# Feed-forward by seven products for each two-by-two block, with its inner activations held in DRAM

## What is computed

```python
hn = _rmsnorm(h, norm_ffn_w[l])
h = h + jnp.square(jax.nn.relu(hn @ w_ffn_in[l])) @ w_ffn_out[l]
...
return _rmsnorm(h, norm_final_w)
```

## Time and profile before

| | |
|---|---|
| median of 3 runs | 2551.32 us (2548.46 to 2555.57) |
| the profiled execution | 2553.9 us, of which the trace's span is 2552.1 us |
| granted TensorE clock over the span, share of full speed | 0.972 |
| PE, PEld busy | 2441.5 us (96%), 2077.6 us (81%) |
| DVE, ACT, POOL busy | 1002.2, 723.1, 689.7 us |
| instructions | 33188 |
| DMA | 232.11 MB, mean 91 GB/s |

### The profile page before, as it was taken

The page is one execution under the profiler, slowest core; times in us unless marked ns, Lnnn a source line. Parts: engine busy times, 40 slices in busy tenths (PEclk is TensorE's granted clock), DMA queues, the critical chain, the costliest instruction groups (busy, mean ns, idle before and its releaser), DMA issues.

```text
span 2552.1 us, 33188 instructions
## 1 busy us (share of the span) xinstructions
PE 2441.5 (96%) x13182; PEld 2077.6 (81%) x13182; DVE 1002.2 (39%) x1479; ACT 723.1 (28%) x1147; POOL 689.7 (27%) x423
## 2 busy tenths in 40 slices
PE   6999996899898999999999999999999999999997
PEld 5788886899876888888888877988888788887886
DVE  4176634455535312212213344123333343557533
ACT  4144554122412100101101121135443113655022
POOL 2221112343322433333334322321111231111321
PEclk8999997899898999999999989999999999999998
DMA  6722212322330111111111115523441346524422
GB/s 206 205 58 67 67 51 68 92 57 57 133 107 25 58 50 42 49 49 49 49 49 49 47 35 187 169 62 91 120 118 51 130 165 145 134 65 149 149 91 91
DMA packets 257967, 232.11 MB, mean 91 GB/s; under 512 B 43233, under 2 KB 228359, under 8 KB 256312
## 3 DMA queue, kind: packets, MB, share of 16 engines
q1 hardware_dynamic: 234680, 170.65, 23.7%
q10 hardware_dynamic: 23168, 59.81, 6.5%
HBM read 167.41 MB, written 65.11 MB: 91 GB/s over the span
## 4 chain that ended last, share of the span: by engine, by line
PE 92%; DVE 2%; ACT 1%; DMA 1%; issue 1%; POOL 1%; POOLq 0%; ACTq 0%; DVEq 0%; SPq 0%; PEldq 0%; PEld 0%
PE PS L282 40%; PE PS L301 18%; PE PS L1828 4%; PE PS L2478 3%; PE PS L418 3%; PE PS L1783 3%; PE PS L2034 2%; PE PS L1320 2%; PE PS L1326 2%; PE PS L698 1%; PE PS L2023 1%; PE PS L2317 1%; PE PS L676 1%; PE PS L1337 1%; PE PS L686 1%
## 5 line engine op out<-in xcount | busy, mean ns | idle before, releaser
L253 POOL CAST Wh<-Wraw 128x1024 fp32r<-128x1024 f32 x144 | 150.8, 1047 | 1469.0 <-PE PS L282 619.3
L255 POOL TENSOR_TENSOR Wl<-Wraw,Wh 128x1024 fp32r<-128x1024 f32 x144 | 375.6, 2608 | 20.7
L1702 ACT ACTIVATE rbuf<-PS 128x1024 f32<-128x1024 f32 x32 | 32.9, 1028 | 493.7 <-PE PS L282 483.2
L282 PE MATMUL PS<-Fl,Wh 128*128 128x512 f32 x512 | 157.6, 389 | 0.0
L282 PE MATMUL PS<-Fh,Wh 128*128 128x512 f32 x512 | 157.6, 389 | 0.0
L282 PE MATMUL PS<-Fh,Wl 128*128 128x512 f32 x512 | 157.6, 389 | 0.0
L282 PE MATMUL PS<-XAh,Wh 128*128 128x512 f32 x440 | 139.7, 399 | 13.0 <-POOL Wl L255 6.0
L301 PE MATMUL PS<-XAh,Wh 128*128 128x512 f32 x328 | 134.8, 411 | 2.1 <-POOL Wl L255 2.1
L282 PE MATMUL PS<-XAl,Wh 128*128 128x512 f32 x440 | 136.1, 391 | 0.0
L282 PE MATMUL PS<-XAh,Wl 128*128 128x512 f32 x440 | 135.9, 390 | 0.0
L282 PE MATMUL PS<-XBh,Wh 128*128 128x512 f32 x440 | 135.5, 389 | 0.0
(11 more groups left out here) (431 smaller groups left out, 5416.4 us busy)
## 6 DMA issues: line engine op xcount, KB each, us to landing
Wraw<-in_w_in SPq DMA_DIRECT2D x66, 512.0 KB, 4.4
Wraw<-in_w_ffn_in SPq DMA_DIRECT2D x32, 512.0 KB, 4.0
Wraw<-in_w_ffn_out SPq DMA_DIRECT2D x32, 512.0 KB, 4.0
x_scr<-hT SPq DMA_DIRECT2D x2, 4096.0 KB, 14.2
Wraw<-in_w_out SPq DMA_DIRECT2D x16, 512.0 KB, 4.1
gate_scr<-gbuf ACTq DMA_DIRECT2D x16, 512.0 KB, 2.6
gin<-gate_scr ACTq DMA_DIRECT2D x8, 1024.0 KB, 7.3
xtok<-in_x SPq DMA_DIRECT2D x4, 1024.0 KB, 8.3
```

The lines of the kernel that those rows point to most:

```text
L253: pool.tensor_copy(Wh[:, slot], Wraw[:, slot])
L255: pool.tensor_tensor(Wl[:, slot], Wraw[:, slot], Wh[:, slot].bitcast(F32), ALU.subtract).then_inc(w_ready, 1)
L282: mm = pe.matmul(PS[:, 2 * slot + b, :], w[:, slot, k], x[:, b * 512:(b + 1) * 512], start=(c == 0 and m == 0), stop=(c == len(xs) - 1 and ...
```

## The change

The feed-forward no longer uses the 64 tiles. Its matrices are cut into two-by-two blocks: an output block is 256 features (two tiles of 128, index f) by two halves of 512 tokens, and the summed index goes in pairs of tiles (even and odd, index e). For each pair, seven products of 128x128 weights with 128x512 activations take the place of eight, each still as three matmuls. They need sums of the weights (four per group, on POOL), sums of the activations (four per pair, on DVE) and sums of the results (partly by accumulation in shared banks, partly on ACT and DVE).

The work goes in 35 groups. Groups 0 to 15 each make one inner block, 256 inner features over all 4 pairs of k. It is squared, written as four 128x512 pieces to `f_scr` in DRAM, 1 MB per group. Groups 16 to 34 are the second product: group 16 + t makes a part of output block t mod 4 from the inner blocks t-3 to t (so one, two, three, then four pairs, and three, two, one at the end), and adds it to `hT`. Each inner block comes back from DRAM, gets its sums and its split while the group before runs, and is kept for four groups: four sets of operands, in turn. Each set holds seven high and seven low tiles of 128x512.

The order is written out without loops: `SEQ` has group by group the products 1, 6, 2, 7, 5, 4, 3; the first two groups alternate, while DVE and ACT make the operands of each product from the normalised `hT`. `hT` itself is written to `x_scr` beforehand, is then normalised in place, and is read back in two parts. Six banks are used, three for even and three for odd groups. Weights come as up to 1 MB per group; ACT makes their high part and POOL the low part, in four slots, so three products ahead. On SP all transfers are put in one list, sorted by keys.

The diff, cut to its core:

```diff
+        HID, OUT = FF // (2 * P), D // (2 * P)
+        KP = 4
+        PROD = (1, 6, 2, 7, 5, 4, 3)
+        BANK = {1: 0, 2: 0, 6: 1, 7: 1, 4: 1, 5: 2, 3: 2}
+        OPENS = (1, 6, 5)
+        NG = HID + HID + OUT - 1
...
+        SEQ = [(g, i) for i in range(7) for g in range(2)] + [(g, i) for g in range(2, NG) for i in range(7)]
...
+        base = [92, 32, 60, R]
...
+        fin = sb("fin", [P, 5, 512], F32, R + 60)
...
+        def prepared(g, i):
+
+            k = g - HID + 1
+            if not 0 <= k < HID:
+                return None, ()
+            first = 4 if k == 0 else 1
+            return k, (range(first + 1) if i == first else (i,) if i > first else ())
...
         def sp_phase7(sp):
-            load_range(sp, N_FFN + 2, N_FOX + 2)
...
+            todo = [(at[g - 2, 6] - 2.5, "weights", g) for g in range(2, NG)]
+            todo += [(at[g, 6] + 1.5, "store", g) for g in range(HID)]
+            todo += [(15, "residual", 0), (at[HID, 1], "residual", 1)]
+            todo += [(at[HID - 2, 6] + 4, "load", 0), (at[HID - 1, 6] + 3, "load", 1)]
+            todo += [(at[HID + k - 2, 3] + 1.2, "load", k) for k in range(2, HID)]
+            todo += [(at[2 * HID - 1, 6] + 2, "next", 0)]
...
+                elif what == "load":
+                    if x < 2:
+                        sp.wait_ge(f_out[x], 8 * HID)
+                    if x:
+                        sp.wait_ge(o_lo, 28 + 7 * (x - 1) + 4)
+                    load_f(sp, x)
...
         def pool_phase7(pool):
-            split(pool, N_FFN + 2, N_FOX + 2)
+            for n, (g, i) in enumerate(SEQ):
+                p = PROD[i]
+                if p == 1:
+                    pool.wait_ge(fw_in[g % 2], 16 * (g // 2 + 1))
+                    pool.drain()
+                    pool.tensor_tensor(wsum[g == 1][:, 0:len(kpairs(g))], wt(g, 1, 0), wt(g, 1, 1), ALU.add).then_inc(fw_sum, 1)
+                    pool.drain()
+                    pool.tensor_tensor(wt(g, 1, 0), wt(g, 0, 0), wt(g, 1, 0), ALU.subtract).then_inc(fw_sum, 1)
+                elif p == 6:
...
+                elif p == 3:
...
+                pool.wait_ge(fw_hi, n + 1)
+                m = len(kpairs(g))
+                pool.tensor_tensor(fw_l[:, n % NS, 0:m], w_source(g, i), fw_h[:, n % NS, 0:m].bitcast(F32), ALU.subtract
+                                   ).then_inc(fw_lo, 1)
...
         def pe_phase7(pe):
...
+            for n, (g, i) in enumerate(SEQ):
+                p, ks = PROD[i], kpairs(g)
+                if p == 1 and g >= 2:
+                    pe.wait_ge(f_dve, dve_reads[g - 2, 2])
+                elif p == 2:
+                    pe.wait_ge(f_act, g + 1)
...
+                elif p in (7, 4, 3):
+                    pe.wait_ge(f_dve, dve_reads[g, {7: 1, 4: 3, 3: 4}[p]])
+                pe.wait_ge(fw_lo, n + 1)
+                if HID <= g < 2 * HID:
+                    pe.wait_ge(o_lo, 28 + 7 * (g - HID) + i + 1)
+                dst = PS[:, 3 * (g % 2) + BANK[p]]
+                for j, k in enumerate(ks):
+                    if g == 0:
+                        pe.wait_ge(o_lo, 4 * i + j + 1)
+                    wh, wl = fw_h[:, n % NS, j], fw_l[:, n % NS, j]
+                    xh_, xl_ = op_h[k % KP][:, i], op_l[k % KP][:, i]
+                    for m, (w, x) in enumerate(((wh, xh_), (wh, xl_), (wl, xh_))):
+                        mm = pe.matmul(dst, w, x, ...)
+                mm.then_inc(f_mm, 1)
...
         def act_phase7(act):
+            def high_w(n):
+                g, i = SEQ[n]
+                p, m = PROD[i], len(kpairs(g))
+                if n >= NS:
+                    act.wait_ge(f_mm, n - NS + 1)
+                act.wait_ge(fw_in[g % 2], 16 * (g // 2 + 1))
+                if p in (6, 7, 5, 3):
+                    act.wait_ge(fw_sum, sums_made[g, p])
+                act.activation(fw_h[:, n % NS, 0:m], w_source(g, i), ACT.Copy).then_inc(fw_hi, 1)
...
+            def high_f(k, i):
...
+                act.activation(op_h[k % KP][:, i], f_source(k, i), ACT.Copy).then_inc(o_hi, 1)
...
+            for n, (g, i) in enumerate(SEQ):
+                if g == 0 and i < 6:
+                    high_x(i + 1)
+                if n + NS - 1 < len(SEQ):
+                    high_w(n + NS - 1)
+                if PROD[i] == 1:
+                    act.wait_ge(f_mm, n + 1)
...
+                    act.activation(dst, PS[:, 3 * (g % 2)], ACT.Copy).then_inc(f_act, 1)
+                k, ops = prepared(g, i)
+                for x in ops:
+                    high_f(k, x)
...
         def dve_phase7(dve):
+            def sums(k):
+                f = sums_of(k)
+                b22 = fin[:, 3 + k % 2]
+                dve.wait_ge(f_in, 64 * (k + 1))
+                dve.tensor_tensor(f[:, 0], fin[:, 1], fin[:, 0], ALU.subtract).then_inc(o_sum, 1)
+                dve.drain()
+                dve.tensor_tensor(f[:, 1], b22, f[:, 0], ALU.subtract).then_inc(o_sum, 1)
+                dve.tensor_tensor(fin[:, 1], b22, fin[:, 1], ALU.subtract).then_inc(o_sum, 1)
+                dve.drain()
+                dve.tensor_tensor(f[:, 2], fin[:, 2], f[:, 1], ALU.subtract).then_inc(o_sum, 1)
+            def low_f(k, i):
+                dve.wait_ge(o_hi, 28 + 7 * k + i + 1)
+                dve.tensor_tensor(op_l[k % KP][:, i], f_source(k, i), op_h[k % KP][:, i].bitcast(F32), ALU.subtract
+                                  ).then_inc(o_lo, 1)
+            def read(n, g, i):
+                p = PROD[i]
+                bank_ = PS[:, 3 * (g % 2) + BANK[p]]
+                dve.wait_ge(f_mm, n + 1)
+                dve.drain()
...
+                if p in (6, 7):
+                    dve.wait_ge(f_act, g + 1)
+                    dve.tensor_tensor(v6 if p == 6 else v7, v1, bank_, ALU.add).then_inc(f_dve, 1)
+                    return
...
+                v = {5: v7, 4: v1, 3: v6}[p]
+                dve.tensor_tensor(v, v, bank_, ALU.add).then_inc(f_dve, 1)
+                dve.drain()
+                if g < HID:
+                    dve.scalar_tensor_tensor(v, v, 0.0, v, ALU.max, ALU.mult).then_inc(f_done, 1)
+                else:
...
+                    ins = dve.tensor_tensor(h, h, v, ALU.add)
...
+            for n, (g, i) in enumerate(SEQ):
+                if g == 0 and 1 <= i < 6:
+                    prep_x(i + 1)
+                if PROD[i] != 1:
+                    read(n, g, i)
+                k, ops = prepared(g, i)
+                if len(ops) > 1:
+                    sums(k)
+                for x in ops:
+                    low_f(k, x)
```

More of the change, by code:

```diff
@@ new lines, in build @@
+        fraw = [sb(f"fraw{x}", [P, 2 * KP, 2 * P], F32, R + 28 + 8 * x) for x in range(2)]
+        NS = 4
+        fw_h, fw_l = sb("fw_h", [P, NS, KP, P], F32R, R + 44), sb("fw_l", [P, NS, KP, P], F32R, R + 52)
+        wsum = [sb("wsum0", [P, KP, P], F32, K0 + 1), sb("wsum1", [P, KP, P], F32, 88)]
+        blocks = [sb(f"blocks{x}", [P, 4, 512], F32, R + 60 + 8 * x) for x in range(2)]
+        C11, C12, C21, C22 = range(4)
+        u1 = sb("u1", [P, 512], F32, R + 76)
+        u6, u7 = sb("u6", [P, 512], F32, 88), sb("u7", [P, 512], F32, 90)
@@ new lines, in build @@
+        fin = sb("fin", [P, 5, 512], F32, R + 60)
+        fsum, fsum0 = sb("fsum", [P, 3, 512], F32, R + 70), sb("fsum0", [P, 3, 512], F32, 24)
+        hdiag = sb("hdiag", [P, S], F32, R + 72)
+        f_scr = dram("f_scr", [HID, 4, P, 512])
+        fw_in = [late_sem("ffn_w_in0"), late_sem("ffn_w_in1")]
+        fw_sum, fw_hi, fw_lo, f_mm, f_act, f_dve, u_used = [late_sem("ffn_" + x) for x in (
+            "w_sums", "w_hi", "w_lo", "products", "first_copied", "banks_read", "first_used")]
+        o_raw, o_sum, o_hi, o_lo = [late_sem("ffn_op_" + x) for x in ("rows", "sums", "hi", "lo")]
@@ L1664, in pe_phase7 @@
-            hidden = [(k, Fh[:, k], Fl[:, k]) for k in range(8)]
-            def second(q):
-                pe.wait_ge(f_ready, q * 8 + 7)
-                pe.sem_inc(f_taken, 1)
-                def last_tile(k, q=q):
-                    if k == 7:
-                        pe.wait_ge(f_ready, q * 8 + 8)
-                with pe.Fori(0, 4) as i:
-                    for s in range(2):
-                        product(pe, q * 16 + i * 2 + (N_FFN + 8 + s), (N_FFN + s) % 2, hidden, last_tile if s == 0 else None)
@@ L1677, in pe_phase7 @@
-            product_two(pe, N_FFN, model, lambda k: pe.wait_ge(x_ready, 9 + k + 2), True)
-            with pe.Fori(0, 3) as i:
-                for s in range(2):
-                    product(pe, i * 2 + (N_FFN + 2 + s), (N_FFN + s) % 2, model)
-            second(0)
-            with pe.Fori(0, 3) as q:
-                with pe.Fori(0, 4) as i:
-                    for s in range(2):
-                        product(pe, q * 16 + i * 2 + (N_FFN + 16 + s), (N_FFN + s) % 2, model)
-                second(q + 1)
@@ L1706, in act_phase7 @@
-            with act.Fori(0, 3) as q:
-                first(q)
-            first(3)
-            for j in range(8):
```

(39 more changed lines are left out.)

232 lines of the change are left out of this document (174 added, 58 removed).

## The result

The changed kernel takes 2599.63 us, median of 4 runs (2596.34 to 2602.09), beside 2553.45 (2548.46 to 2556.82) for the kernel before in the same comparison: 1.0182 times as long, 95% interval 1.0159 to 1.0204. That is 46 us slower where 35 were forecast. The profiled execution took 2601.13 us, its span 2599.4.

What follows compares the result with a forecast made beforehand. TensorE, busy 96% of the span, was taken as the bound. 615.6 + 26 + 33 + 40 + 23 = 737.6 us in place of 703.05, 35 longer, gave 2588 us; own range 2555 to 2625, 8 in 10 2540 to 2640.

Steps and rivals of the forecast that it cites:

- the port: DVE operations with two SBUF operands and POOL's operations exclude each other, so their times add; chance 0.58, 2555 to 2625.
- Matmuls: Whole feed-forward: 2688 matmuls in place of 3072, at 0.229 us each, 615.6 us (609 to 645).
- The first product at no cost: First product's groups: port work of 15.4 us stays under TensorE's 19.2 per group, so TensorE stays the bound.
- The second product: Twelve prepared groups with four pairs: 22.0 us each against 19.2 of matmuls, 33 us lost (0 to 105).
- The total of 21.5 us at the port: Second product, per group: 11 POOL operations at 1.13 plus 14 DVE operations at 0.65, over TensorE's 19.2.
- The ramp: First two groups, worked alternately while DVE makes the operands: 26 us lost, between 6.6 and 40.
- put at nothing: Block writes and reads, residual reload, next stage's weight tiles loaded and split: no cost; if late, 5 to 7 us.
- Between the products: Start of second product: block store and load, then DVE's work for short groups; 40 us lost (15 to 55).
- The end: Last two groups, paced by DVE's reads and additions of squares, then column sums: 23 us (5 to 30).
- Hidden after all: Rival: POOL idles during DVE's sums, groups run at TensorE's 19.2 and short groups recover; 2510 us, chance 0.15.
- Strict alternation: Rival: each DVE operation meets a fresh POOL operation, 26 us per second-product group; 2637 us, chance 0.17.
- Clock: Rival: pauses at bank reads bring TensorE to 1.2 GHz, 29 us over 12 groups; 2618 us, chance 0.10.

Runs made afterwards that it cites:

- version 1: Changed kernel with VectorE's seven low parts per inner block subtracting a PSUM bank instead of the SBUF high part (computation not kept): 2562.5 us.
- version 11: Changed kernel with low parts subtracting a PSUM bank (computation not kept) and POOL making the next group's first two weight sums early: 2560.9 us.
- version 9: Changed kernel plus PSUM copies, early block return, late weight split, early weight sums, ScalarE's high parts first, spare eviction buffer and smaller order edits: 2544.7 us.
- version 3: Changed kernel with inner blocks 0 and 1 read back early in the first product and summed there, residual read back in three parts: 2585.7 us.
- version 10: Changed kernel without VectorE's twelve additions of squares at the end of the feed-forward, all semaphores kept: 2591.3 us.
- version 4: Changed kernel with POOL's split of the next stage's two weight tiles waiting for VectorE's last squares: 2597.4 us.
- version 2: Changed kernel with ScalarE's second high part one step later and VectorE reading product 7 before product 2, no work removed: 2611.5 us.

## Why the prediction was right

The time, 2599.6, lies in the forecast's own range, and by its mechanism: the port is the larger part of the steady loss, and the rest lies where I had put it, in the ramp, between the products and at the end. Term by term:

*Matmuls.* 2688 at 0.229 us; 0.2292 measured.

*The first product at no cost.* Right: its matmuls from 873.22 on run without a pause in the profile, 1155 at 19.25 us per group, with POOL busy for 76% of the time.

*The second product, 22.0 us per group and 33 in all.* 22.27 and 36.5. The walk through one group named both of TensorE's waits: product 4 "0.3 late" for the read of product 7 (measured 1.41), and product 6 for POOL's low part (0.81). DVE's low parts, forecast near a mean of 1.2 us, took 1.20 from `fin` and 1.62 from sums (1250 to 1430). That two engines add up at the port is shown by version 1; that some of it is the queues' order, by version 11. The total of 21.5 us at the port, counted as bound, was nearly the group; but the port was not all of it: 22% of the loss went with an order alone once the lock was off. That 21.5 stands so near is in part luck: in the earlier trace rows the subtraction ends 1.09 us after POOL's operation, not the 1.2 that I read, and here 0.54 to 0.55 for half the width. With 0.55 for each of DVE's 14 operations the sum is 20.1.

*The ramp, 26.* 28.6. What I had not seen is a wait of 3.82 us of TensorE for the eviction of group 2, which waits for the store of block 0 (chain of waits):

```profile
868.13 4.35 DMA f_scr<-blocks
...
872.57 0.61 ACT blocks L1870
```

It is one of the transfers that I had put at nothing; a spare buffer in version 9 took that wait away.

*Between the products, 40.* 38.2, with the store, the load and the sums in that order on the path (16 us, version 3), and DVE's surplus in the short groups behind them. The 6 us of matmuls at the lower clock level stood in no term.

*The end, 23.* 31.4, the term that was mis-sized. What follows the last sum was right: from its end at 1543.60 to the root it takes 18.5 us, where I had 18.7. The additions of squares were on the path, as I had them: 15.0 us in version 10, the split's delay of them included, where I had two groups of 7.5. But I had the sums end 17 us late, and they end 24.0 late (198 matmuls at 0.229 from 1474.28 on would end at 1519.6). Of these 7 us 4.9 are the split of the next stage's weights, which I had put at nothing and which holds the port against the last additions and sums (version 4); the other 2 stay open. I had charged the lock to the steady groups and not asked for it where the two engines meet next.

The four differences, 2.6, 3.5, -1.8 and 8.4, make the 12.7 us by which the stage is longer than forecast (750.3 in place of 737.6).

*Rivals.* Hidden after all: its condition, that fewer of DVE's operations meet POOL's, is what version 11 makes true, half of the 14 being left, and there the group is TensorE's 19.3. Strict alternation: not reached; of 63 low parts the 27 from sums took 1347 ns or more, but half of the other 36 under 1030. Clock: 0.99 in the steady groups, whose pauses are 0.81 and 1.41 us; it was lower in the stretches with longer holes, 0.88 in the ramp, 0.75 between the products, 0.94 in the last groups, and 0.50 behind the last matmul.

## What to carry to other kernels

Before work is moved to an engine that is "only 27% busy", list which of its operations and of its neighbour's read two operands from SBUF, and add those up per period: here the sum passed TensorE's period, and the twelve steady groups lost 36 us. That is not the whole bill. 87 us of saved matmuls became 46 us of loss, and of the 135 us lost the ramp, the change from one product to the other and the end took 98: count each of these by what has to be done there in a row. An operand in PSUM takes an operation out of that sum, but whatever puts it there stands in another queue. When the resource is free, the order of the queues decides, one wait after another, and each is read from the row of the waiting product and the rows ahead of it in its releaser's queue.

## What the runs showed of the hardware

POOL pays for the lock as well: in the changed kernel's steady groups a two-input operation of 128x512 takes 1.27 to 1.29 us where it comes first, and mostly 1.54 to 1.55 or 1.72 to 1.82 elsewhere (four in a row took 1.24 each). And a reordering that adds no work made DVE 14.5 us in 180 busier (version 2): here busy time holds the waits for the port, so a busier engine need not be doing more.
